# Overlapping an attention with the projection before it and the output tiles behind it

## What is computed

```python
def _neighbourhood_attention(q, k, v, k_ctx, v_ctx, rel_bias):   # one_row, for each row of 64 queries
        s_nb = jnp.einsum('bqhd,bjhd->bhqj', q_row, k_rows).astype(jnp.float32) * scale + bias[None]
        s_nb = jnp.where(mask[None, None], s_nb, NEG)
        s_cx = jnp.einsum('bqhd,bjhd->bhqj', q_row, k_ctx).astype(jnp.float32) * scale
        p = jax.nn.softmax(jnp.concatenate([s_nb, s_cx], axis=-1), axis=-1).astype(v.dtype)
        return (jnp.einsum('bhqj,bjhd->bqhd', p[..., :n], v_rows)
                + jnp.einsum('bhqj,bjhd->bqhd', p[..., n:], v_ctx))

def _odd_mixer(h, hc, w_in, w_out, q_g, k_g, rel_bias, ctx_out):
    q, k, v = split(h @ w_in)          # split also norms q and k per head
    qc, kc, vc = split(hc @ w_in)
    o = _neighbourhood_attention(q, k, v, kc, vc, rel_bias) @ w_out
```

## Time and profile before

| what | value |
|---|---|
| median of three runs | 2153.16 us |
| lowest, highest | 2150.04 us, 2582.49 us |
| profiled execution | 2153.89 us, its span 2152.1 us |
| mean granted TensorE clock | 0.989 of full speed |
| TensorE, VectorE, ScalarE, POOL busy | 96%, 70%, 45%, 15% of the span |
| first attention, first scores to first output tile | 155.97 to 207.84 us |
| second attention, end of the value projection to first output tile | 765.10 to 831.91 us |

### The profile page before, as it was taken

How to read it: one execution, slowest core, us unless ns; L and a number is a source line. 1 busy time by engine, 2 the same in 40 slices (tenths; PEclk the granted TensorE clock), 3 DMA queues, 4 the chain that set the end, 5 groups by cost and what they waited for, 6 DMA issues and landing times.

```text
span 2152.1 us, 34724 instructions
## 1 busy us (share of the span) xinstructions
PE 2074.6 (96%) x12633; PEld 1772.4 (82%) x12633; DVE 1499.1 (70%) x2685; ACT 975.7 (45%) x1545; POOL 321.9 (15%) x340
## 2 busy tenths in 40 slices
PE   7998999999989988999999999999999999999998
PEld 3755778888878757999999988999988888888887
DVE  4535578894247745665597867997986677777776
ACT  3426332222234355444469535446743444444444
POOL 0114000000004021000000006787830000000000
PEclk8999999999999999999999999999999999999999
DMA  8352345694226303455554534551256655555553
GB/s 290 118 179 88 108 146 190 209 327 143 98 79 177 100 9 102 149 180 186 174 176 162 201 128 144 171 183 54 69 166 216 198 192 186 192 188 188 190 188 117
DMA packets 92896, 342.18 MB, mean 159 GB/s; under 512 B 10383, under 2 KB 10399, under 8 KB 92272
## 3 DMA queue, kind: packets, MB, share of 16 engines
q1 hardware_dynamic: 89280, 325.10, 45.0%
q0 software_dynamic: 3504, 15.56, 2.5%
HBM read 339.57 MB, written 1.05 MB: 158 GB/s over the span
## 4 chain that ended last, share of the span: by engine, by line
PE 89%; DVE 4%; ACT 3%; issue 2%; DMA 1%; POOL 0%; SPq 0%; DVEq 0%; ACTq 0%; POOLq 0%
PE banks L1015 20%; PE banks L1455 16%; PE banks L1064 9%; PE banks L1421 7%; PE banks L1333 6%; PE banks L1204 5%; PE banks L1424 3%; PE banks L1382 3%; PE banks L942 2%; PE banks L1366 2%; PE banks L1104 2%; PE banks L1029 2%; PE banks L968 1%; PE banks L1217 1%; PE banks L764 1%
## 5 line engine op out<-in xcount | busy, mean ns | idle before, releaser
L1015 PE MATMUL banks<-act_parts,first_w_parts 128*128 128x512 f32 (+1 forms) x2544 | 464.0, 343 | 3.1 <-DVE ffn_hidden_parts L2050 1.8
L1015 PEld LDWEIGHTS banks<-act_parts,first_w_parts 128*128 128x128 f32 x2544 | 400.4, 190 | 64.0 <-issue 7.3
L1455 PE MATMUL banks<-w_parts,a_parts 128*128 128x512 f32 x1524 | 360.4, 390 | 0.1
L2050 DVE TENSOR_TENSOR first_w_parts<-weight_ring,first_w_parts 128x1024 fp32r<-128x1024 f32 x166 | 206.8, 1248 | 207.0 <-ACT first_w_parts L1635 206.9
L1455 PEld LDWEIGHTS banks<-w_parts,a_parts 128*128 128x128 f32 x1524 | 285.9, 188 | 59.4 <-issue 0.8
L2050 DVE TENSOR_TENSOR w_parts<-weight_ring,w_parts 128x1024 fp32r<-128x1024 f32 x207 | 253.7, 1226 | 74.3 <-ACT w_parts L1635 71.8
L1635 ACT ACTIVATE w_parts<-weight_ring 128x1024 fp32r<-128x1024 f32 x207 | 218.9, 1058 | 184.0 <-PE banks L1421 102.1
L1635 ACT ACTIVATE first_w_parts<-weight_ring 128x1024 fp32r<-128x1024 f32 x166 | 174.8, 1056 | 236.1 <-PE banks L1015 124.1
L1421 PE MATMUL banks<-n_parts,w_parts 128*128 128x512 f32 x632 | 229.4, 397 | 1.3 <-DVE w_parts L2050 1.3
L1064 PE MATMUL banks<-ffn_hidden_parts,first_w_parts 128*128 128x512 f32 (+1 forms) x1056 | 183.4, 336 | 0.0
L1064 PEld LDWEIGHTS banks<-ffn_hidden_parts,first_w_parts 128*128 128x128 f32 x1056 | 162.5, 190 | 20.6
(11 more groups left out here) (315 smaller groups left out, 2903.8 us busy)
## 6 DMA issues: line engine op xcount, KB each, us to landing
weight_ring<-in_stream SPq DMA_DIRECT2D x618, 512.0 KB, 3.3
main_zone<-in_rel_bias POOLq DMA_DIRECT2D x6, 512.0 KB, 11.7
rounded<-in_dft_input POOLq DMA_DIRECT2D x1, 1600.0 KB, 7.5
rounded<-in_dft_inverse POOLq DMA_DIRECT2D x1, 1280.0 KB, 6.1
main_zone<-in_xT POOLq DMA_DIRECT2D x1, 1024.0 KB, 12.6
main_zone<-in_ctxT POOLq DMA_DIRECT2D x1, 1024.0 KB, 17.7
main_zone<-in_c_rows POOLq DMA_DIRECT2D x1, 1024.0 KB, 6.9
tail_zone<-in_rel_bias POOLq DMA_DIRECT2D x2, 512.0 KB, 24.2
```

The source lines that it names most:

```text
L1015: mm = pe.matmul(o[:, 0:w], wb[:, hw, k, :], fin[:, hx, k, 0:w], start=(k == 0 and n == 0), stop=(k == DC - 1 and n == 2))
L1455: mm = pe.matmul(acc[n][:, :], ap_[:, e % 3, ha, (n // 2) * P:(n // 2 + 1) * P], wp[(B + b) % PARTS][:, hw, (n % 2) * 512:(n % 2 + 1) * 51 ...
L2050: return dve.tensor_tensor(o, a, b, op)
```

## The change

- `scores` is taken out of `attention` and called for units 0, 1 and 2 of the second attention in the second half of the value projection, behind its weight blocks 0, 1 and 2. The banks of the projection are chosen anew so that 0 and 1 are free for scores. ScalarE's exponents for these units stand ahead of its copies of the second half's V rows. VectorE's low part of the last projection block stands behind the minima of unit 0. The attention's own loop begins with the transposes of unit 0 and then round 3.
- In both attentions the order in a round becomes scores(i), transposes(i-2), values(i-3) on TensorE, and copies(i-2), exponents(i) on ScalarE.
- Transposed probabilities take turns between two pairs of banks in the first attention (2, 3 and from unit 3 on 6, 7 for odd units), and between three banks (3, 7, 6) in the second. For that the adaptation sums in banks 6 and 7 are copied out in round 3.
- Probabilities and their transposes of the second attention lie in other places of SBUF (`att_of`, `pt_of`), in scratch of the head norms and in buffers of used weight blocks.
- The first output tile (`out_part`) is made in pieces of three matmuls, some of them among the last three rounds; only its last piece waits for the last unit's output. The wait for all of `o_copied` is gone.
- ScalarE's first two high parts for the output tiles go to rounds 9 and 10, VectorE's two low parts to rounds 13 and 14.

```diff
-        VBANKS = [[3, 6, 7, 2], [0, 1, 3, 6]]
+        VBANKS = [[6, 2, 3, 7], [4, 5, 6, 2]]
@@ TensorE, v_by_token
+                    if h == 1 and kb < 3:
+                        if kb == 0:
+                            pe.wait_ge(qk_normed, QKN[0] + QKN[1])
+                        scores(1, kb)
@@ TensorE, attention
-                pe.wait_ge(vt_copied, [1, 9][l])
+                pe.wait_ge(vt_copied, [1, 5][l])
@@ turn
-                        if i >= 1:
-                            pe.wait_ge(pt_copied, 2 * (u0 + i - 1) + half + 1)
+                        n = turned_last(l, i, half)
+                        if n is not None:
+                            pe.wait_ge(pt_copied, 2 * u0 + n + 1)
+                        elif i:
+                            pe.wait_ge(*[(ada_rows_copied, 4), (vt_copied, 9)][l])
@@ the loop
-                for i in range(PAIRS + 3):
+                if l == 1:
+                    turn(0)
+                for i in range(3 * l, PAIRS + 3):
                     if i < PAIRS:
-                        scores(i)
+                        scores(l, i)
                         for f in fill[l][(1 - l) * EARLY:][i * GROUP:(i + 1) * GROUP]:
                             ada(*f)
+                    if 0 <= i - 2 < PAIRS:
+                        turn(i - 2)
+                    if i >= PAIRS:
+                        out_part(l, AHEAD_OF_VALUES[l][i - PAIRS])
                     if 0 <= i - 3 < PAIRS:
                         values(i - 3)
-                    if 0 <= i - 2 < PAIRS:
-                        turn(i - 2)
-                pe.wait_ge(o_copied, u0 + PAIRS)
+                out_part(l, range(AHEAD_OF_VALUES[l][-1][-1] + 1, DC - 1))
+                if l == 0:
+                    ada_turn(1)
+                out_part(l, [DC - 1])
+
+            AHEAD_OF_VALUES = [[(0,), (1,), (2,)], [(0,), (1, 2), (3,)]]
@@ out_part, for each piece c
+                    if c < MIXC[l]:
+                        pe.wait_ge(four_split, c + 1)
+                    else:
+                        pe.wait_ge(o_copied, l * PAIRS + (c - MIXC[l] + 1) * ATT[l]["qt"])
+                    for n, (hw, hx) in enumerate(TERMS):
+                        mm = pe.matmul(o[:, 0:w], wb[:, hw, c, :], fin[:, hx, c, 0:w],
+                                       start=(c == 0 and n == 0), stop=(c == DC - 1 and n == 2))
@@ ScalarE, attention
+                if l == 1:
+                    for i in range(3):
+                        exponents(i)
+                    v_rows_out(1, (0, 1))
+                    v_rows_out(1, (2, 3))
+                    turned_out(0)
+                for i in range(3 * l, PAIRS + 2):
+                    if i in (9, 10):
+                        if l == 0:
+                            high("ev_out", i - 9, None, owp)
+                        else:
+                            high_out(i - 9)
+                    if 0 <= i - 2 < PAIRS:
+                        turned_out(i - 2)
+                    if l == 0 and i == 3:
+                        ada_copy(1)
                     if i < PAIRS:
+                        exponents(i)
@@ VectorE, attention
-                if l == 1:
-                    evacuated(dve, "od_in", 16)
-                    dve.wait_ge(w_lo, ORD["od_in"] + 24)
                 for i in range(PAIRS + 3):
+                    if l == 1 and i == 1:
+                        low("od_in", 23)
+                    if l == 1 and i == 2:
+                        dve.wait_ge(w_lo, ORD["od_in"] + 24)
...
-                        if j >= PAIRS - PARTS + 1:
+                        if j in (10, 11):
                             if l == 0:
-                                low("ev_out", j - (PAIRS - PARTS + 1), None, owp)
+                                low("ev_out", j - 10, None, owp)
                             else:
-                                low_out(j - (PAIRS - PARTS + 1))
+                                low_out(j - 10)
```

More of the change, by code:

```diff
@@ L155 @@
 ATT0 = 34816
+FWP0 = 34816
 FOUR0 = 17408
@@ L612, in build @@
         MIXC = [4, 0]
-        att = view(ATT0, 4, 2, 514)
-        att_pt = view(ATT0 + 4 * 2 * 514, 2, 2, 4, P)
         mask_e = view(MASKE0, QT, T)
@@ L927, in v_turn, with scores @@
                 mm.then_inc(vt_ready, 1)
+            def scores(l, i):
+                pr, us, u0 = projections[l], pairs(l), l * PAIRS
+                pair, qt = us[i]
+                qc, kc = [(4 + pair, 8), (pair, 8 + pair)][l]
+                n = keys_of(l, qt)
+                for half in range(2):
+                    if i >= 1:
+                        pe.wait_ge(rowmin_ready, 2 * (u0 + i - 1) + half + 1)
+                    pe.matmul(bank[half][:, 0:n], pr[head(half), qc, qt * P:(qt + 1) * P], pr[head(half), kc, T - n:T],
+                              start=True, stop=True).then_inc(scores_ready, 1)
             def v_by_token(h):
                 for tt, b in enumerate(VBANKS[h]):
-                    if b < LB:
+                    if h == 0 and b < LB:
                         pe.wait_ge(tile_free, max(n for n in range(TILE["od_in"] + 16) if n % LB == b) + 1)
-                    elif h == 1:
+                    if h == 1 and b not in VBANKS[0]:
+                        pe.wait_ge(qk_std, QKN[0] + QKN[1])
+                    if h == 1 and b in VBANKS[0]:
                         pe.wait_ge(vt_copied, 1 + VBANKS[0].index(b) + 1)
@@ L956, in attention @@
                     pe.wait_ge(qk_ready, 1)
-                else:
-                    pe.wait_ge(qk_normed, QKN[0] + QKN[1])
-                pe.wait_ge(vt_copied, [1, 9][l])
-                def scores(i):
-                    pair, qt = us[i]
-                    qc, kc = [(4 + pair, 8), (pair, 8 + pair)][l]
-                    n = keys_of(l, qt)
-                    for half in range(2):
-                        if i >= 1:
-                            pe.wait_ge(rowmin_ready, 2 * (u0 + i - 1) + half + 1)
-                        pe.matmul(bank[half][:, 0:n], pr[head(half), qc, qt * P:(qt + 1) * P], pr[head(half), kc, T - n:T],
-                                  start=True, stop=True).then_inc(scores_ready, 1)
+                pe.wait_ge(vt_copied, [1, 5][l])
                 def turn(i):
@@ L1097, in _ @@
             attention(0)
-            pe.wait_ge(four_split, 4)
-            for m in range(DC):
+            for m in range(1, DC):
                 wb = split_block(ORD["ev_out"] + m, None, owp)
@@ L1745, in _ @@
             attention(0)
-            ada_copy(1)
             before_ffn(0)
@@ L1760, in _ @@
             v_rows_out(0)
-            for b in (22, 23):
-                high("od_in", b)
-            v_rows_out(1)
+            high("od_in", 22)
+            high("od_in", 23)
             attention(1)
@@ L2186, in qk_norm @@
                 for j, (c, w, g, sq_at, r_at) in enumerate(CHUNKS[l]):
-                    while split < min(count, first + j + lag + PARTS + 1):
+                    while split < min(count - l, first + j + lag + PARTS + 1):
                         low(name, split)
@@ L2200, in qk_norm @@
                     last.then_inc(qk_normed, 1)
-                for b in range(split, count):
+                for b in range(split, count - l):
                     low(name, b)
@@ L2245, in attention @@
                                 u = 2 * (u0 + i) + half
-                                s, sink = att[:, i % 4, half], par("sink", pair + 4 * half)
+                                s, sink = att_of(l, i, half), par("sink", pair + 4 * half)
                                 dve.wait_ge(scores_ready, u + 1)
```

88 lines of the change are left out of this document (54 added, 34 removed).

## The result

The changed kernel takes 2135.79 us (median of five runs, 2134.16 to 2140.98); the kernel before, in five runs, 2153.07. One of these five, at 2582.49, stands far outside the others and is left out of the ratio. The ratio is 0.9935, 95% interval 0.9925 to 0.9946: 14.0 us less, or 0.65% (the two medians lie 17.3 us apart). A second series, with six runs of it and eleven of before, gave 0.9943 (0.9930 to 0.9956), 12.2 us less. By the bound of 2% it is no change; the intervals show that it is a small gain. The profiled execution took 2134.16 us, with a span of 2132.3.

What follows compares the result with a forecast made beforehand. TensorE, busy 96% of the 2152.1 us span, was taken as the bound. The second attention's stretch falls from 69.7 to 57.6 us (12.1 less), the first gains 1.0: 13.1 less, median 2140.1 us, range 2133 to 2148.

Steps and rivals of the forecast that it cites:

- (c): Second attention, units 3 to 15: 13 rounds bound by TensorE at 3.11 us each, 40.4 us, against 3.53 a round before.
- (a): Value projection's second half: scores of units 0 to 2 among weight blocks cost about 1.3 us each, 3.9 us.
- (b): End of the value projection: unit 0 transposed at once, with a change of operands, 1.3 us.
- (d), (e): Second attention's end: two transposes and three values 5.1 us, first tile's 24 matmuls 2.9, four operand changes 1.0.
- (f): Second attention, rounds 13 and 14: VectorE's low parts overload it, so transposes of units 13 and 14 wait, 2.0 us.
- (g): Second attention: VectorE's low parts and POOL's scaling share an SBUF port; 1.0 us, between nothing and 3.8.
- lock in both directions: Rival: POOL also waits for VectorE's splits, 2.8 us more in each attention, 2145.7 us; chance 0.08.
- the 0.4 for the rounds in which POOL splits the Fourier half: First attention: exponents of units 2 and 3, behind copies, lose up to 1.0 us, of which 0.4 taken.
- Rounds of 3.5: Rival, second attention: rounds don't get shorter, as exponents wait for copies; 5.5 us lost, 2145.6 us; chance 0.15.
- scores that stretch the projection: Rival, value projection: each of three scores waits about 2.0 us for minima, 6 us more, 2146 us; chance 0.05.
- late reciprocals: Rival, second attention: reciprocals fall a round late on VectorE, 5.9 us a round, up to 2176.5 us; chance 0.04.
- Better: Case: no VectorE overload or port cost felt and the first attention gives 4 us, 2134 us; chance 0.08.

Runs made afterwards that it cites:

- late_scores: Changed kernel with scores of units 0 to 2 of the second attention behind the value projection again; two runs, 2137.46 and 2138.99 us.
- old_order: Changed kernel with the second attention's rounds in the earlier order, values ahead of transposes and exponents ahead of copies; 2143.47 us.
- changed again: The changed kernel unaltered, profiled a second time; 2136.14 us.

## Why the prediction came out as it did

The forecast was 2140.1, with 12.1 us less in the second attention and 1.0 in the first. Measured were 2135.79, and 14.0 and 0.3: in all 14.3 for 13.1. The other 3 us of the median's distance from the forecast lie in no term; the start of the program alone scatters by 6. The largest term, (c), held. The second attention by its terms (the changed kernel's trace, us):

| term | predicted | measured | from |
|---|---|---|---|
| (a) scores in the projection | 3.9 | 3.8 | 6.74 a block against 5.48, three times |
| (b) first transposes | 1.3 | 0.9 | 762.76 to 763.66 |
| (c) 13 rounds | 40.4 | 40.4 | 3.11 each |
| (d), (e) last units, tile, changes of operands | 9.0 | 8.6 | 804.95 to 814.71, less 1.19 of waiting |
| (f), (g) waits late in the attention | 3.0 | 2.1 | 0.90 in round 14, 1.19 behind the last |
| sum | 57.6 | 55.8 | before 69.7 |

- **(a)** held to 0.1: a neighbouring row, an insertion of the same kind elsewhere, was enough to price an operation that the trace didn't have. What went wrong is the other side: I said that an uncovered unit "would cost the 3.4 us that start-up units cost now". The 3.4 was taken at the lower clock. At full clock the uncovered units cost 2.5, and the early scores themselves 3.3 us in all (late_scores); another 3 is the clock, which stayed up where the 0.78 us of waiting were missing. The sum was not touched, as it was laid out from the new sequence and the clock's loss lay in the 69.7.
- **(c)** The limit was in the order and not in an engine's load. old_order shows it: 3.54 a round with everything else in place.
- **(d), (e)** Sized right, the reason half right. The time came from covered copies and from each piece's own wait, not from placing pieces among the rounds. The changes of operands, of which there are six and not four, cost 0.3 to 0.6 and not 1.0.
- **(f)** The step that failed by its cause. I had both waits from VectorE's overload. The one in round 14 is POOL held up by the low part; only the last is VectorE's queue, half of it the low part. That (f) and (g) together came to 2.1 for 3.0 is in part luck: their causes were shared out wrongly.
- **(g)** The rival of a lock in both directions had 0.08 and is what happens, at about a third of its price: POOL meets one of the two low parts, and TensorE had slack for part of it. That costs 0.9 us in the second attention and about as much in the first (a wait of 0.98), where I had 2.8 more in each. For a pair of engines that was seen to hold each other up in one order, the other order was the likelier guess, and its cost hangs on where in the round they meet, which was to be laid out beforehand.
- **First attention.** The gains came: 0.5 in rounds 3 to 5, 0.5 of the 0.7 in the pattern from unit 8 on, and from unit 12 to the tile 1.1 (25.06 to 23.94). The term that failed is the 0.4 for the rounds in which POOL splits the Fourier half: it was 1.8 (6.48 to 8.30), 1.4 for the queue and some 0.5 for the clock, which the forecast did not see falling here. I had seen POOL busy 12.74 of 13.4 us and took that as "nothing is gained there". The new order has values wait behind the very transposes that wait for POOL, so what was covered became exposed.
- **The rivals.** Rounds of 3.5, scores that stretch the projection and late reciprocals did not come: no wait stands in rounds 3 to 13. "Better" (2134) was 1.8 from the median, yet its reason was wrong: (f) and (g) are both felt.

How the gain of the second attention divides, by the runs: order of the rounds 4.5, early scores 3.3, clock about 3.2 (14.38 less 11.18), the wait ahead of the first scores, gone with the new choice of banks, 0.8, and the end, last scores to second tile: 15.47 before, 13.30 in old_order, so 2.2 that the order doesn't hold. That is all of the 14.0. The terms of the prediction don't show this, as its 69.7 holds the clock's loss and the 0.78 without a name. The kernel before, run again, lost 0.5 less to the clock and took 113.58; the rest is its other rhythm of the same rounds.

## What to carry to other kernels

When an engine's queue is reordered, list for each moved instruction what now stands behind it, and ask whether its releaser is an engine with other work in its queue; here one change of order earned 4.5 us where the releaser was free and lost 1.4 us where POOL was splitting, 1.8 with the clock that fell behind the wait. Before work is interleaved to fill a gap, look whether waits taken apart do it alone: a tile behind the rounds with a wait per piece beat the one spread among them. Price a start-up by rows at the clock that the changed kernel will have, and compare by stretches between marks where the start of the program scatters by more than the effect.

## What the runs showed of the hardware

- POOL's scaling of two halves (128 x 512, float32) takes 1.36 us alone and 2.42 to 2.43 where a VectorE subtraction of two SBUF operands (1.22 us) falls between the halves. With the earlier trace rows either engine is seen held up by the other. Starting POOL 0.8 us sooner removed it.
- TensorE's clock fell to its lower level (granted 0.50) in both runs of the kernel before, behind idle stretches of 0.78 and 1.38 us with 1.13 us of matmuls between. Behind idle stretches of 1.38 and 0.93 it stayed at 1.00 in both runs of late_scores. The penalty was about 3 us. What decides is open.
- The same code with the same waits (1.17 and 0.97 us) can keep the clock or lose it: in the first attention old_order kept it, and four runs of the same code there (changed, changed again, late_scores twice) had it at 0.50 for 3.4 us, at a price of 0.4 to 0.9 us.
- The 150 us ahead of the first attention, code that is the same in all kernels, took 149.85 to 156.00 us in 14 profiled executions.
